# Four split activation buffers of a two-layer decoder trunk: 272 words instead of 264 from one contraction tile to the next

## What is computed

```python
def _mixer(h, S0, buf0, pos, w_in, w_out, ...):
    z = h @ w_in                       # 2048 -> 7168
    q, k, v, g_r, a, b, g_c = jnp.split(z, SPLITS, axis=-1)
    ...                                # rotary, 8 heads of chunked retention, group norm
    ret_out = o.astype(h.dtype) * jax.nn.silu(g_r)
    u = a * jax.nn.sigmoid(b)          # causal depthwise convolution of width 31, layer norm
    ...
    c = c @ w_pw2 + b_pw2              # 1024 -> 1024
    conv_out = c * jax.nn.silu(g_c)
    m = jnp.concatenate([ret_out, conv_out], axis=-1) @ w_out     # 2048 -> 2048

    # in _trunk, for each layer i
    hn = _rms_norm(x, g_pre[i])
    m, S, buf = _mixer(hn, ...)
    h = x + _rms_norm(m, g_post[i])
    e = _rms_norm(p[i] @ w_ple[i], g_ple[i])                      # 256 -> 2048
    x = h + jax.nn.sigmoid(h @ w_ple_gate[i]) * e                 # 2048 -> 2048
```

## Time and profile before

| | |
|---|---|
| runs | 1272.76, 1274.84, 1275.97 us; median 1274.84 |
| profiled execution | 1272.7 us span; the device time is the same stretch, first to last instruction, and the three runs are the only times given |
| granted TensorE clock, mean | 0.987 |
| busy: TensorE, VectorE, ScalarE, GpSimd | 1218.1, 919.9, 613.6, 136.4 us |
| DMA | 225.71 MB, mean 177 GB/s |

### The profile page before, as it was taken

One profiled execution on the slowest core, in us unless ns is written; L12 is line 12 of the kernel. 1 busy time (PEld: TensorE's weight loads), 2 busy tenths in 40 slices (PEclk: granted clock), 3 DMA queues, 4 the chain that ended last, 5 costly groups with the idle time before them and its releaser, 6 DMA issues.

```text
span 1272.7 us, 25528 instructions
## 1 busy us (share of the span) xinstructions
PE 1218.1 (96%) x9814; PEld 1195.9 (94%) x9814; DVE 919.9 (72%) x1404; ACT 613.6 (48%) x952; POOL 136.4 (11%) x188
## 2 busy tenths in 40 slices
PE   5999999999999999889998999999999999997998
PEld 5999899999989999789998999999999999996998
DVE  6798898888976532477868879988889764326673
ACT  6342555555546444635544335555554554455341
POOL 0000011112100012401110000211111000123000
PEclk9999999999999999989999999999999999997999
DMA  7555654454543553515554565555544445533462
GB/s 266 189 211 189 191 198 170 180 198 174 211 148 141 202 194 118 182 69 197 198 196 170 199 204 193 182 194 191 192 167 167 154 176 186 182 117 132 152 224 89
DMA packets 42595, 225.71 MB, mean 177 GB/s; under 512 B 6176, under 2 KB 12320, under 8 KB 18976
## 3 DMA queue, kind: packets, MB, share of 16 engines
q1 hardware_dynamic: 28800, 201.47, 44.6%
q10 hardware_dynamic: 13728, 23.33, 5.5%
HBM read 210.97 MB, written 13.81 MB: 177 GB/s over the span
## 4 chain that ended last, share of the span: by engine, by line
PE 81%; DVE 9%; issue 4%; ACT 3%; POOL 1%; DMA 1%; ACTq 0%; POOLq 0%; DVEq 0%; SPq 0%
PE ps L424 24%; PE ps L425 23%; PE ps L426 23%; DVE wlo L940 3%; PE ps L487 2%; DVE acc L1247 1%; ACT whi L637 1%; PE ps L517 1%; PE ps L518 1%; PE ps L519 1%; DMA raw<-w_in 1%; DVE tmp L1025 1%; POOL acc L1416 1%; DVE c_buf L1025 1%; PE ps L479 0%
## 5 line engine op out<-in xcount | busy, mean ns | idle before, releaser
L424 PE MATMUL ps<-a_hi,whi 128*128 128x264 f32 x2112 | 612.7, 290 | 27.0 <-DVE wlo L940 13.7
L425 PE MATMUL ps<-a_lo,whi 128*128 128x264 f32 x2112 | 600.9, 285 | 0.0
L426 PE MATMUL ps<-a_hi,wlo 128*128 128x264 f32 x2112 | 600.4, 284 | 0.0
L940 DVE TENSOR_TENSOR wlo<-raw,whi 128x2048 fp32r<-128x2048 f32 x192 | 435.5, 2270 | 217.0 <-ACT whi L637 214.8
L424 PEld LDWEIGHTS ps<-a_hi,whi 128*128 128x128 f32 x2112 | 400.0, 189 | 39.0 <-issue 21.8
L637 ACT ACTIVATE whi<-raw 128x2048 fp32r<-128x2048 f32 (+1 forms) x188 | 351.4, 1873 | 150.2 <-DMA raw<-w_in 71.3
L425 PEld LDWEIGHTS ps<-a_lo,whi 128*128 128x128 f32 x2112 | 400.6, 190 | 0.1
L426 PEld LDWEIGHTS ps<-a_hi,wlo 128*128 128x128 f32 x2112 | 398.5, 189 | 0.0
L424 PE MATMUL ps<-b_hi,whi 128*128 128x264 f32 x672 | 191.1, 284 | 1.6 <-ACT tmp L899 1.6
L425 PE MATMUL ps<-b_lo,whi 128*128 128x264 f32 x672 | 190.4, 283 | 0.0
L426 PE MATMUL ps<-b_hi,wlo 128*128 128x264 f32 x672 | 190.3, 283 | 0.0
(11 more groups left out here) (186 smaller groups left out, 1196.3 us busy)
## 6 DMA issues: line engine op xcount, KB each, us to landing
raw<-w_in SPq DMA_DIRECT2D x112, 1024.0 KB, 4.9
raw<-w_out SPq DMA_DIRECT2D x32, 1024.0 KB, 4.8
raw<-w_gate SPq DMA_DIRECT2D x32, 1024.0 KB, 4.8
s_new<-s_ret ACTq DMA_DIRECT2D x16, 512.0 KB, 5.5
ss_out<-s_new ACTq DMA_DIRECT2D x16, 512.0 KB, 2.9
raw<-w_pw SPq DMA_DIRECT2D x8, 1024.0 KB, 4.8
raw<-w_ple SPq DMA_DIRECT2D x8, 512.0 KB, 3.6
x<-x_t SPq DMA_DIRECT2D x4, 528.0 KB, 9.4
```

Of the source, the lines that this page charges most:

```text
L424: pe.matmul(accum[bank][:, 0:R], whi[:, slot, w:w + P], hi, start=k == 0, stop=False)
L425: pe.matmul(accum[bank][:, 0:R], whi[:, slot, w:w + P], lo, start=False, stop=False)
L426: mm = pe.matmul(accum[bank][:, 0:R], wlo[:, slot, w:w + P], hi, start=False, stop=k == k_tiles - 1)
L940: v.tensor_tensor(wlo[:, slot, 0:cols], raw[:, slot % RAW, 0:cols], whi[:, slot, 0:cols].bitcast(F32), ALU.subtract).then_inc(s.lo_ready, 1)
```

## The change

The four buffers `a_hi`, `a_lo`, `b_hi` and `b_lo` keep 264 rows in each contraction tile, but the tiles stand 272 words apart. Tile k of `a_hi` then starts at 83072 + 1088 k, at a multiple of 64 for every k, and the other three again at the same place modulo 256. That takes 4 x 512 bytes more of each partition. To make room, `sq` (2112 bytes) no longer has memory of its own and lies where `gz` and `sg` lie. What stood behind the buffers moves by +2048 bytes, what stood behind `sq` by -64, so each keeps its place modulo 64. `c_hi` and `c_lo` keep their tiles 264 words apart. Every view of the four buffers is cut to its 264 rows; `operand` replaces `rows` where they are written one tile at a time. No instruction is added, taken out or moved on TensorE, ScalarE, GpSimd or SyncE, and every wait stays; VectorE computes three more addresses in registers, in the loop at lines 1377 of before. Operations that cover several contraction tiles of these buffers have one more dimension (128x4x264 instead of 128x1056).

```diff
+PITCH = 272
...
-    a_hi = sb("a_hi", [P, KT, R], F32R)
-    a_lo = sb("a_lo", [P, KT, R], F32R)
-    b_hi = sb("b_hi", [P, KT, R], F32R)
-    b_lo = sb("b_lo", [P, KT, R], F32R)
-
-    c_buf = sb("c_buf", [P, CT, R], at=sb_at["b_hi"][0] + CT * R * 4)
-    gc_buf = sb("gc_buf", [P, CT, R], at=sb_at["b_lo"][0] + CT * R * 4)
+    a_hi = sb("a_hi", [P, KT, PITCH], F32R)
+    a_lo = sb("a_lo", [P, KT, PITCH], F32R)
+    b_hi = sb("b_hi", [P, KT, PITCH], F32R)
+    b_lo = sb("b_lo", [P, KT, PITCH], F32R)
+
+    c_buf = sb("c_buf", [P, CT, R], at=sb_at["b_hi"][0] + CT * PITCH * 4)
+    gc_buf = sb("gc_buf", [P, CT, R], at=sb_at["b_lo"][0] + CT * PITCH * 4)
...
-    sq = sb("sq", [P, 2, R])
...
+    sq = sb("sq", [P, 2, R], at=sb_at["gz"][0])
...
+    def operand(t, tile):
+
+        return t[:, :, :].rearrange("p k r -> p (k r)")[:, bass.ds(tile * PITCH, R)]
...
-        in_a = lambda k: (a_hi[:, k, :], a_lo[:, k, :])
-        in_b = lambda k: (b_hi[:, k, :], b_lo[:, k, :])
+        in_a = lambda k: (a_hi[:, k, 0:R], a_lo[:, k, 0:R])
+        in_b = lambda k: (b_hi[:, k, 0:R], b_lo[:, k, 0:R])
...
-                nc.scalar.activation(b_hi[:, 4 * g:4 * g + 4, :], x[:, 4 * g:4 * g + 4, :],
+                nc.scalar.activation(b_hi[:, 4 * g:4 * g + 4, 0:R], x[:, 4 * g:4 * g + 4, :],
...
-                nc.scalar.activation(rows(a_hi, t), rows(x, t), ACT.Copy,
+                nc.scalar.activation(operand(a_hi, t), rows(x, t), ACT.Copy,
...
-            v.scalar_tensor_tensor(rows(a_lo, t), rows(x, t), vec(l, t + V_PRE), rows(a_hi, t).bitcast(F32),
+            v.scalar_tensor_tensor(operand(a_lo, t), rows(x, t), vec(l, t + V_PRE), operand(a_hi, t).bitcast(F32),
                                    ALU.mult, ALU.subtract).then_inc(s.xin_ready, 1)
...
-            group = lambda t, g: t[:, 4 * g:4 * g + 4, :]
+            group = lambda t, g: t[:, 4 * g:4 * g + 4, 0:R]
```

More of the change, by code:

```diff
@@ L755, in ret_round @@
             act.wait_ge(s.rt_ready, h + (HEADS * l + 1))
-            nc.scalar.activation(rows(b_hi, h - 1), rt[:, :], ACT.Copy).then_inc(s.rhi_ready, 1)
+            nc.scalar.activation(operand(b_hi, h - 1), rt[:, :], ACT.Copy).then_inc(s.rhi_ready, 1)
         def channel_silu(l, c):
@@ L775, in _ @@
             for k in range(4 * g, 4 * g + 4):
-                nc.scalar.activation(a_hi[:, k, :], x[:, k, :], ACT.Copy,
+                nc.scalar.activation(a_hi[:, k, 0:R], x[:, k, :], ACT.Copy,
                                      scale=vec(0, V_PRE + k)).then_inc(s.xhi_ready, 1)
@@ L847, in _ @@
             act.wait_ge(s.p_in, 16 * (l + 1))
-            nc.scalar.activation(a_hi[:, CT:CT + PT, :], p_in[:, :, :], ACT.Copy).then_inc(s.phi_ready, 1)
+            nc.scalar.activation(a_hi[:, CT:CT + PT, 0:R], p_in[:, :, :], ACT.Copy).then_inc(s.phi_ready, 1)
             for j in range(4):
@@ L852, in _ @@
                     act.wait_ge(acc_free[e], read_out_at(l, T_W // 2 + j))
-                    nc.scalar.activation(a_hi[:, 2 * j + e, :], gc_buf[:, 2 * j + e, :],
+                    nc.scalar.activation(a_hi[:, 2 * j + e, 0:R], gc_buf[:, 2 * j + e, :],
                                          ACT.Copy).then_inc(s.cohi_ready, 1)
@@ L1097, in ret_lo @@
             dve.wait_ge(s.rhi_ready, h + HEADS * l)
-            v.tensor_tensor(rows(b_lo, h - 1), rt[:, :], rows(b_hi, h - 1).bitcast(F32),
+            v.tensor_tensor(operand(b_lo, h - 1), rt[:, :], operand(b_hi, h - 1).bitcast(F32),
                             ALU.subtract).then_inc(s.ret_ready, 1)
@@ L1316, in _ @@
                     dve.wait_ge(s.phi_ready, l + 1)
-                    v.tensor_tensor(a_lo[:, CT:CT + PT, :], p_in[:, :, :], a_hi[:, CT:CT + PT, :].bitcast(F32),
+                    v.tensor_tensor(a_lo[:, CT:CT + PT, 0:R], p_in[:, :, :], a_hi[:, CT:CT + PT, 0:R].bitcast(F32),
                                     ALU.subtract).then_inc(s.pin_ready, 1)
@@ L1321, in _ @@
                     dve.wait_ge(s.cohi_ready, CT * l + c + 1)
-                    v.tensor_tensor(a_lo[:, c, :], gc_buf[:, c, :], a_hi[:, c, :].bitcast(F32),
+                    v.tensor_tensor(a_lo[:, c, 0:R], gc_buf[:, c, :], a_hi[:, c, 0:R].bitcast(F32),
                                     ALU.subtract).then_inc(s.cout_ready, 1)
```

## The result

The changed kernel took 1281.35 us (median of 20 runs, 1277.68 to 1287.59), the kernel before 1278.09 us in the 20 runs beside it (1272.76 to 1282.36). The ratio is 1.0036, with a 95% interval of 1.0023 to 1.0048. The forecast was 0.5% faster, the range ended at 1277. Set against the 1274.84 us that the prediction started from, the ratio gives 1279.4 us, 2.4 us above the range.

The account below looks back on a forecast made before the run. TensorE's warm split matmuls, 8310 intervals of mean 120.85 ns, were taken to bound the kernel. Odd starts gave 5.8 us less, all else 0: 1266.9 us profiled, median 1269.0 us, range 1260 to 1277.

Parts of the forecast that it names:

- What bounds the kernel: TensorE's split matmuls: 8310 warm intervals, mean 120.85 ns, hold 1004 us; one nanosecond per interval is 8.3 us, or 0.65%.
- the operand's start sets the pattern: Split matmuls: the repeat after 8 tiles fits the moving operand's start; even k take 120.16 ns, odd k 121.55.
- broken rows: VectorE and ScalarE operations spanning several buffer tiles: taken as 0, bound 2.1 us for each engine if wholly bare.
- squares: `sq` placed on `gz` and `sg`: no wait is added, taken as 0.
- the register work: VectorE's two-pass loop of the gate stage, first layer: three more register computations per pass, at most 2.3 us, taken as 0.
- the first item of the sum: Split matmuls over `a` and `b`: odd k starts run as even k do, 0.70 ns x 8310 = 5.8 us less.
- The lower bound of the price: Split matmuls: k = 0, 4, 8, 12 take 119.25 ns, so at best 1.6 x 8310 = 13.3 us less.
- The upper bound: Split matmuls: if all run like odd k, 121.55 ns, 0.70 x 8310 = 5.8 us more.
- The rival "slower": Split matmuls: operand and weight reads meeting modulo 64 disturb each other, now always; +5.8 us, 1280.6 us, chance 0.12.
- The 106 ns of the one-column matmuls: Line 487's 16 one-column matmuls: about 106 ns each, read as the cost of loading weights and changing over alone.
- the 121.5 ns of the pointwise product: Product over `c`, 384 matmuls keeping 264 words: 121.5 ns read from a 35.00 us window, 0 change.
- Forecast of the proof: Window from 430 us: 582 or 583 starts instead of 579, repeat after 4 tiles; product 121.5, cold 220, one-column 106 ns.

Follow-up runs that it names:

- the probe: The kernel before with 25 streams of 96 warm split matmuls behind its last output tile, varying starts, weights and columns; 295 us of streams, read by their intervals.
- the squares alone: The kernel before, pitch still 264, with only `sq` moved onto `gz`'s memory and what stood behind it by 2112 bytes; ratio 1.0003 (0.9988 to 1.0017).

## Why the prediction was wrong

*What bounds the kernel* held: one interval repeated 8300 times carries four fifths of the span, and 1 ns of it is worth 0.65%. *That the operand's start sets the pattern* held: it repeats after four tiles now, and fixed weights changed nothing. Of the things costed at nothing, broken rows (1259 and 1088 ns against 1258 and 1086) and squares (1.0003) were nothing; the register work was not tried by itself, but is in the kernel that came out faster.

*The step that failed* is the first item of the sum: "If they then run as even k do, the mean goes from 120.85 to 120.16 ns". It took each interval's length as a property of its own start. The intervals of a running stream are one rhythm of all its starts together: the even starts alone, in the order they now come, run at 121.11 or 122.78 ns, and the same starts cost 119.3 to 121.7 (k = 0, 2, 4 and 6 of the prediction's own list) when odd ones lay between them. The lower bound of the price (119.25 ns) was wrong for the same reason, and its "kind" k = 0, 4, 8, 12 holds two different starts modulo 256, those of k = 0 and k = 4; no stream of 264 columns ran below 120.00 in any steady stretch. The upper bound, 121.55, was below the slower rhythm. The term was taken at -0.70 ns and measured +0.82 and +0.71 in two profiles.

The rival "slower" had the sign, and with +5.8 us nearly the interval's price of 5.9 to 6.8, but its mechanism is refuted: it blamed starts that agree with the weights modulo 64. A fixed start at 0 modulo 64 gave 120.0 ns in one stream and 16 bytes beside it gave 120.0 as well, and the old step 16 bytes later, whose starts never agree with the weights modulo 64, ran slower (121.42 ns) than when half of them did. The text had the sign of trouble in hand: "k = 3 is as fast as any even one and k = 2 is slower". In the rule of the Trainium skill (TensorE: Matmul & The Clock Gate, Part 2) that weight loads take nothing from the running matmul, the prediction saw an interval independent of the start. The runs show start-dependent intervals from 120.0 to 126.7 ns; they don't test the rule itself.

*Two readings.* The 106 ns of the one-column matmuls is a mean of unlike intervals: of the fifteen between the sixteen starts, fourteen are 111 or 112 ns and one is 27 or 28. So what such a matmul with new weights takes is 111.7 ns, as with 128 and 192 columns in the probe, and that is above the 110 ns of 264 columns. What lies on top of the longer of the two is some 9 ns. And the 121.5 ns of the pointwise product came from a window with other tiles in it; its own intervals had 121.75. What in the chip produces the excess isn't settled: that the two reads disturb each other was only argued.

*Forecast of the proof* mostly held: the pointwise product stayed (121.77), cold matmuls stayed at 220 ns. The window held 570 starts instead of the 582 forecast.

*Sizes.* Intervals ask for 1.0046 to 1.0053 and 1.0036 (1.0023 to 1.0048) was measured, and most of the experiments measured 0.001 to 0.002 below what their intervals ask for (the squares alone and 268 words agree). The mean granted clock of each run accounts for much of this. Of the 73 runs of the kernel before that stand beside the experiments, the 22 with a mean clock up to 0.982 have a median of 1278.8 us and the 30 from 0.986 on 1274.9: some 0.7 us per 0.001. The twelve runs of each layout that starts 16 bytes later have a mean clock of 0.9862, the 22 of the kernel before beside them 0.9837, which is worth 1.8 us or 0.0014. At equal clock, an estimate from these numbers, the new step 16 bytes later is some 2.6 us faster than the kernel before (4.4 by the mean times as they are), where its intervals ask for 1.9, and the old step 16 bytes later some 4.5 us slower (2.7), where they ask for 4.8. The changed kernel's twenty runs have 0.9875; the clock of the runs beside them isn't on record. Whether a layout changes how long TensorE runs cold, or chance did, stays open. So does what it is at a restart that chooses the rhythm: the width of a lead-in matmul chose it reproducibly, but the kernel's own waits were not varied.

## What to carry to other kernels

When a kernel is one interval repeated thousands of times, don't average the interval's own variation by kind and expect a kind to keep its mean when it stands alone; put the exact sequence of operands behind the kernel as a stream of its own, behind several lead-ins, and read its rate. Here that gave the kernel's rate to 0.1 ns for both layouts that start 16 bytes later (the old step behind one start-up only), and missed by 0.6 and 1.0 ns for 268 and 276 words, seen once each and with half of the kernel's starts. Prefer a layout that falls into the same rhythm behind every lead-in over one that is fast behind some, and change start offset and step separately: with the new step 16 bytes of offset turned a loss of 0.36% into a gain of 0.36%, of which the intervals account for 0.15%, and with the old step the same 16 bytes made the interval 0.57 ns longer.

## What the hardware showed that was not expected

- Warm, back-to-back 128x128 float32r matmuls with new weights each never ran at their columns' time: 264 columns took 120.0 ns at best (110.0 by columns), 320 took 146.7 (133.3), 512 took 226.7 (213.3). 192 and 128 columns both took 111.7 ns, and one-column matmuls that load new weights 111 to 112.
- The interval depends on the moving operand's start: 120.0 ns at 16 bytes from the buffer's start, 126.7 at 96 (one stream each), and in whole kernels 120.85 ns with 264 words, 121.42 with the same starts 16 bytes later.
- A stream can have several rhythms (for 272-word steps 120.54, 121.1 and 122.8 ns). The last two held for tens of microseconds in the kernel and changed at a restart; a step of 264 words had one, behind twelve lead-ins and in every undisturbed tile of its kernel's profile.
